# Expert lookup of a hybrid encoder block: one gather of a U row and a V row together instead of two gathers of single rows

## What is computed

```python
        ue = jnp.take(u, it, axis=0)
        act = jax.nn.gelu(jnp.einsum("td,tkd->tk", xt, ue), approximate=False) * gt
        ve = jnp.take(v, it, axis=0)
        return jnp.einsum("tk,tkd->td", act, ve)
```

## Time and profile before

| | before |
|---|---|
| median of 3 runs | 1613.03 us (1610.24 to 1615.33) |
| the profiled execution, its own time | 1609.72 us |
| its span, first to last instruction | 1607.5 us |
| TensorE busy | 1523.1 us (95%) |
| DVE busy | 1426.0 us (89%) |
| ACT busy | 633.5 us (39%) |
| POOL busy | 705.5 us (44%) |
| moved by DMA | 448.19 MB |
| POOL's queue q0 (the gathers) | 57344 packets, 201.42 MB |

### The profile page before, as it was taken

How to read it: one execution, slowest core, us unless ns; L and a number is a source line. 1 busy time by engine, 2 the same in 40 slices (tenths; PEclk the granted TensorE clock), 3 DMA queues, 4 the chain that set the end, 5 groups by cost and what they waited for, 6 DMA issues and landing times.

```text
span 1607.5 us, 22474 instructions
## 1 busy us (share of the span) xinstructions
PE 1523.1 (95%) x7627; PEld 1243.6 (77%) x7627; DVE 1426.0 (89%) x2813; ACT 633.5 (39%) x950; POOL 705.5 (44%) x535
## 2 busy tenths in 40 slices
PE   5999999999999999989999999899899999999997
PEld 3787774675557799978888888788788888888885
DVE  6888876773999899968999999999999999999995
ACT  4235554232113566653333333333233333333333
POOL 0000000001555620006777677677666677778740
PEclk8999999989999999999999999999999999999998
DMA  8432214642221166679999999999999999999991
GB/s 349 166 157 79 79 53 173 221 172 89 89 75 53 61 211 210 216 273 386 411 412 387 410 405 412 410 404 411 359 380 404 392 381 412 404 410 410 408 366 53
DMA packets 127309, 448.19 MB, mean 279 GB/s; under 512 B 13825, under 2 KB 34561, under 8 KB 114561
## 3 DMA queue, kind: packets, MB, share of 16 engines
q1 hardware_dynamic: 68448, 243.21, 40.1%
q0 software_dynamic: 57344, 201.42, 31.9%
q10 hardware_dynamic: 1440, 2.62, 0.4%
HBM read 421.44 MB, written 25.69 MB: 278 GB/s over the span
## 4 chain that ended last, share of the span: by engine, by line
PE 49%; DVE 34%; DMA 6%; issue 6%; ACT 3%; POOL 1%; DVEq 0%; SPq 0%; ACTq 0%
PE ps L911 17%; PE ps L682 10%; PE ps L980 9%; PE ps L673 6%; DVE Us L1881 4%; DVE low L1946 3%; DVE low L1869 3%; PE ps L838 3%; DVE Vs L1898 3%; DMA low<-pu,eidx 3%; DVE low L1911 2%; DVE big L1911 2%; DVE low L1862 2%; DVE As L1902 1%; ACT Vs L1367 1%
## 5 line engine op out<-in xcount | busy, mean ns | idle before, releaser
L911 PE MATMUL ps<-xs,Us 128*128 128x320 f32 x2832 | 452.3, 317 | 42.6 <-DVE Us L1881 40.7
L980 PE MATMUL ps<-Vs,As 128*128 128x512 f32 x2032 | 491.9, 396 | 0.8 <-DVE As L1902 0.8
L911 PEld LDWEIGHTS ps<-xs,Us 128*128 128x128 f32 x2832 | 431.6, 193 | 68.0 <-issue 42.8
L980 PEld LDWEIGHTS ps<-Vs,As 128*128 128x128 f32 x2032 | 388.8, 193 | 75.7 <-issue 1.7
L609 POOL DMA_INDIRECT big<-pv,eidx x192 | 306.9, 1598 | 119.3 <-issue 43.3
L609 POOL DMA_INDIRECT big<-pu,eidx x96 | 141.1, 1469 | 206.0 <-DMA gmat<-big 146.8
L609 POOL DMA_INDIRECT low<-pu,eidx x96 | 147.9, 1540 | 56.8 <-DVE colv L1911 35.5
L1898 DVE TENSOR_TENSOR Vs<-big,Vs 128x1024 fp32r<-128x1024 f32 x127 | 154.9, 1220 | 14.1 <-ACT Vs L1367 14.0
L563 POOL TENSOR_TENSOR xs<-big,xs 128x320 fp32r<-128x320 f32 x8 | 6.6, 858 | 360.0 <-ACT xs L1215 360.0
L1361 ACT ACTIVATE big<-ps 128x320 f32<-128x320 f32 x96 | 42.1, 439 | 296.1 <-PE ps L911 296.1
L673 PE MATMUL ps<-big 128*128 128x512 f32 (+1 forms) x416 | 158.7, 540 | 0.0
(11 more groups left out here) (256 smaller groups left out, 2011.0 us busy)
## 6 DMA issues: line engine op xcount, KB each, us to landing
big<-puT SPq DMA_DIRECT2D x128, 512.0 KB, 6.7
big<-pvP SPq DMA_DIRECT2D x64, 1024.0 KB, 9.9
big<-stream SPq DMA_DIRECT2D x31, 1024.0 KB, 5.0
gmat<-big SPq DMA_DIRECT2D x10, 2048.0 KB, 8.6
graw<-gmat SPq DMA_DIRECT2D x30, 512.0 KB, 11.8
low<-wada SPq DMA_DIRECT2D x28, 512.0 KB, 4.7
work<-wada SPq DMA_DIRECT2D x14, 512.0 KB, 5.3
graw<-gmat SPq DMA_DIRECT2D x15, 256.0 KB, 11.7
```

The source lines that it names most:

```text
L911: mm = nc.tensor.matmul(ps[:, 6 + e, 0:ET], a, xs[:, b, k, :], start=(k == 0 and a is hi and b == 0), stop=(k == KT - 1 and a is lo))
L980: mm = nc.tensor.matmul(ps[:, 2 * b + half, :], a, v_parts[:, w, half * T:(half + 1) * T], start=(opens and i == 0), stop=(last and i == l ...
```

## The change

The host puts U and V side by side (`puv`, 8 KB per expert), and one gather fetches both rows of an expert, 128 partitions x 8 KB, into 4 buffers of 8 KB. There are 192 gathers instead of 384, with the same bytes. The rows are spread over blocks 2 to 126 by `rows_by`, one or two in a block (192 in 125 blocks). In its block a row gets its dot first, ahead of `rest_u`; ACT then applies GELU to the block's one or two columns and multiplies each with its gate (`weigh_rows`, between rounding V and rounding the activations); DVE adds the weighted V rows at the end of the block, behind `weigh`. A buffer is free when its V row has been added.

The 64 head rows are now in one group: 64 tokens x 2 halves of their slots on 128 partitions, one copy of the activations, one sum, one fold. Two DMAs instead of 32 rearrange the gates, and two instead of 32 the indices. POOL issues the first two gathers before `all_stored`. `row_weights` goes; a shorter `folds` comes in block 126, behind that block's additions, and TensorE's fold now waits for it. ACT's turns are written out instead of looped.

```diff
-ROWBUF = 8
+ROWBUF = 4
-XTOK = EXT * NEXT
+XTOK = P // 2
+ROW0, ROW1 = 1, 126
...
+        row = [low[:, 0:2 * D], low[:, 2 * D:4 * D], big[:, 6 * D:8 * D], big[:, 8 * D:10 * D]]
...
+        def rows_by(o):
+            return NROWS * min(max(o - ROW0, 0), ROW1 - ROW0) // (ROW1 - ROW0)
...
-            all_stored(pool)
             pool.wait_ge(g_last, 2)
-            for r in range(2 * NROWS):
+            for r in range(NROWS):
+                if r == 2:
+                    all_stored(pool)
                 fetch(r)
...
                     if last and d == BODY - 2:
                         pe.wait_ge(gel_ready, XT + 2)
-                        pe.wait_ge(row_used, NROWS + XTOK)
-                        for q in range(NEXT):
-                            fold_halves(acc_ext[q], gath[q], begins=(q == 0))
+                        pe.wait_ge(row_used, XTOK)
+                        pe.wait_ge(fold_ready, 4)
+                        fold_halves(acc_ext, gath, begins=True)
...
+            def weigh_rows(r0, r1):
+                act.wait_ge(row_dotted, r1)
+                f(dots[:, r0:r1], dots[:, r0:r1], ACT.Gelu).then_inc(row_gelu, r1 - r0)
+                if r0 == 0:
+                    act.wait_ge(ext_here, 16 * 4)
+                    act.wait_ge(gate_copied, 2)
+                act.wait_ge(row_gelu, r1)
+                for r in range(r0, r1):
+                    f(act_w[:, r:r + 1], act_w[:, r:r + 1], ACT.Copy, scale=dots[:, r:r + 1]).then_inc(row_weighed, 1)
...
+            def add_row(r):
+                dve.wait_ge(row_weighed, r + 1)
+                src, w = row[r % ROWBUF][:, D:2 * D], act_w[:, r:r + 1]
+                dst = acc_ext if r < XTOK else acc[:, r % 2, :]
+                before = r if r < XTOK else r - 1
+                if r in (0, XTOK, XTOK + 1):
+                    i = v.tensor_scalar(dst, src, w, None, ALU.mult)
+                else:
+                    dve.wait_ge(row_used, before)
+                    i = v.scalar_tensor_tensor(dst, src, w, dst, ALU.mult, ALU.add)
+                i.then_inc(row_used, 1)
+
+            def folds():
+                dve.wait_ge(row_gelu, NROWS)
+                dve.wait_ge(row_weighed, NROWS)
+                v.memset(gath[:, XTOK:P], 0.0).then_inc(fold_ready, 1)
+                v.tensor_tensor(gath[:, 0:XTOK], ident[:, 0:XTOK], ident[:, XTOK:P], ALU.add).then_inc(fold_ready, 1)
...
+                    for r in range(rows_by(o - 1), rows_by(o)):
+                        dot(r)
                     if nxt % EVERY != EVERY - 1 and o + 1 < XT:
                         i = nxt - nxt // EVERY
                         rest_u(g * LATE + (EARLY + i), i % 2)
                     weigh(g, d)
-                    for r in range(dots_by(o - 1), dots_by(o)):
-                        dot(r)
-                    if o == UB:
-                        row_weights()
-                    for r in range(adds_by(o - 1), adds_by(o)):
+                    for r in range(rows_by(o - 1), rows_by(o)):
                         add_row(r)
-                    if o == XT - 3:
-                        dve.wait_ge(row_used, 2 * NROWS)
+                    if o == ROW1:
+                        folds()
+                        dve.wait_ge(row_used, NROWS)
                         step(v.tensor_tensor(acc[:, 0, :], acc[:, 0, :], acc[:, 1, :], ALU.add))
                         dve.wait_ge(h_here, 16 * (TB + 1))
```

More of the change, by code:

```diff
@@ L214, in build @@
         As = sb("As", [P, 2, 2 * ET], f32r)
-        nrep = [low[:, (2 + q) * D:(3 + q) * D].rearrange("p (k c) -> p k c", k=KT) for q in range(2)]
-        spread_at = big[:, 8 * D:10 * D].rearrange("p (q d) -> p q d", q=2)
+        nrep = low[:, 2 * D:3 * D].rearrange("p (k c) -> p k c", k=KT)
         Us = sb("Us", [P, 2, 2, D], f32r)
@@ L1268, in _ @@
                 f(n_tok[:, half * T:(half + 1) * T], ps[:, 6 + half, :], ACT.Copy).then_inc(side_free, 1)
[L1270 to L1276, removed]
+            f(nrep.rearrange("p k (q t) -> p k q t", q=2),
+              nT[:, :, P:P + XTOK].unsqueeze(2).broadcast_to([P, KT, 2, XTOK]), ACT.Copy).then_inc(spread_ready, 1)
             def gelu_early(n):
@@ L1319, in _ @@
                     f(graw[:, 1, FILLED - 2, :, :], piece[:, pslot(PIECES - 2), 0:GRUN, :], ACT.Copy).then_inc(g_last, 1)
-                if j == 3:
-                    act.wait_ge(idx_ready, 2)
-                    act.wait_ge(gate_copied, 2)
-                    for q in range(2):
-                        f(n_exts[q], spread_at[:, q, :], ACT.Copy).then_inc(ext_ready, 1)
                 if j == 2:
@@ L1908, in dot @@
                 if r == 0:
-                    dve.wait_ge(ext_ready, NEXT)
+                    dve.wait_ge(ext_ready, 1)
                 row_wait(r)
-                v.tensor_tensor_reduce(out=u_row[r % ROWBUF], in0=u_row[r % ROWBUF],
-                                       in1=n_exts[r // EXT] if r < XTOK else n_tok, scale=1.0, scalar=0.0,
-                                       op0=ALU.mult, op1=ALU.add, accum_out=dots[:, r:r + 1]).then_inc(row_used, 1)
-            def row_weights():
-                dve.wait_ge(row_used, NROWS)
-                step(v.memset(acc[:, 0, :], 0.0))
-                step(v.memset(acc[:, 1, :], 0.0))
-                for q in range(NEXT):
-                    step(v.memset(gath[q], 0.0))
-                settled()
-                for q in range(NEXT):
-                    step(v.tensor_reduce(gath[q][:, q * EXT:(q + 1) * EXT], ident[:, :].rearrange("p (h t) -> p t h", h=PH),
-                                         axis=AX.X, op=ALU.add))
-                dve.wait_ge(gelu_ready, 1)
-                dve.wait_ge(ext_here, 16 * 2 * PH * NEXT)
-                step(v.tensor_tensor(act_w[:, :], act_w[:, :], dots[:, :], ALU.mult))
-                settled()
-                pairs = ident[:, :].rearrange("p (t w) -> p w t", w=2)
-                step(v.tensor_tensor(fold[:, XB:P], pairs[:, 0, :], pairs[:, 1, :], ALU.add))
-                step(v.memset(fold[:, 0:XB], 0.0))
-                settled()
@@ L1935, in add_row @@
[L1935 to L1947 removed]
+                u = row[r % ROWBUF][:, 0:D]
@@ new lines, in dot @@
+                v.tensor_tensor_reduce(out=u, in0=u, in1=n_ext if r < XTOK else n_tok, scale=1.0, scalar=0.0,
+                                       op0=ALU.mult, op1=ALU.add, accum_out=dots[:, r:r + 1]).then_inc(row_dotted, 1)
+            def add_row(r):
[9 more added lines that the diff above has]
+                i.then_inc(row_used, 1)
```

108 lines of the change are left out of this document (30 added, 78 removed).

## The result

The changed kernel takes 1672.55 us (median of 4 runs, 1669.21 to 1677.51), the kernel before 1612.68 in the same comparison (4 runs, 1610.24 to 1615.33): a ratio of 1.038, interval [1.0351, 1.0408]. It is 60 us slower, and outside the predicted range of 1588 to 1640. The profiled execution has a span of 1670.7 us, 63.2 more than before.

What follows compares the result with a forecast made beforehand. DVE's work was taken to set the pace, with TensorE 0.2 us per block behind and gathers just hidden. Seven steps sum to -8.1 us: 1601.6 for a profiled execution, about 1605 for the median; range 1588 to 1640.

Steps and rivals of the forecast that it cites:

- Step 1: Building the matrix: two ACT copies of the head activations go, and DVE's idle time behind them; -2.0 us.
- Step 2: Start of the dense blocks: the first two gathers, issued earlier, compete with the awaited U slice; +4.5 us.
- Steps 3 and 4: Block 62 to 63 without row_weights -5.0, shorter folds +0.9; fewer waits between additions -5.0, rows spread to block 126 -5.
- steps 4 and 5: Dense blocks: row work gains -5.0 by fewer addition waits and -5 by spreading; ACT's single-column work costs +4.
- Step 5: ACT between rounding V and the activations: GELU and single-column multiplications can delay the low part; +4 us, bounds 0 and 9.
- Step 6: The end: three folds go, -4.9, but TensorE idles about 6 us and then loses 2.4; together -2.5 us.
- Step 7: Second row of a two-row block: gather lands in 7.3 us against 7.8 available; +2 us, bounds 0 and 62.
- Rival B: Dot of a two-row block's second row: the buffer loop decides, DVE waits every pair; 1640 or about 1630 us; chance 0.31.
- C: SP's loads: U slices come late beside rows with larger packets; about 1630 us; chance 0.06.
- D: Dense blocks: DMA was the hidden bound, so fewer row bytes per block save 21 us; about 1589 us; chance 0.13.

Runs made afterwards that it cites:

- e_stored: The changed kernel with all gathers behind the wait for the last stores, as before the change; 1676.32 us, ratio 1.039.
- e_onegroup: The kernel before with only the 64 head rows made one group on 128 partitions; gathers, buffers and row_weights stay; 1608.47 us, ratio 0.997.
- e_freedot: The changed kernel with a buffer free at the row's dot and additions reading a resident tile instead of the V row; 1591.74 us, ratio 0.988.
- e_2211: The changed kernel with rows spread 2, 2, 1, 1 by block modulo four instead of 1 and 2 in turn; 1639.29 us, ratio 1.016.
- e_late: The changed kernel with dots behind `rest_u` and the gate product, and ACT's GELU of a row behind its rounding of A; 1638.66 us, ratio 1.015.
- e_all: The changed kernel with rows 2, 2, 1, 1, six buffers from row 84, and dots behind `rest_u` and the product; 1602.94 us, ratio 0.994.

## Why the prediction was wrong, step by step

*Step 1, building the matrix, -2.0.* The store that ends it came at 706.28 instead of 707.40: -1.1. But without the two copies it also came at 708.67 (e_stored) and 711.62 (e_onegroup), so no gain is shown. The idle time that I took for their price did not go with them: DVE still idled 3.37 us at that place, against 3.18.

```profile
559.36 1.23 DVE L1821 TENSOR_TENSOR Us<-big,Us 128x1024 fp32r<-128x1024 f32 x1 [3.37 <-ACT Us L1212]
```

*Step 2, the start, +4.5.* Right in size: 17.0 us from the store to the U slice instead of 13.1, +3.9, and 4.4 by e_stored. Giving it back gained nothing in the total; why is open (e_stored).

*Steps 3 and 4, row_weights and the rows.* From block 62 to 63 it was -3.8, and in e_freedot, where nothing waits for a row, 1134.13 - 1127.12 = 7.01 us, -4.8 against 11.78: as predicted. In e_freedot the other blocks from 3 to 125 gained 10.6 and 4.2 us, 14.8 together, more than the 10 less 4 of *steps 4 and 5*. How it divides between the head additions, the spreading and ACT was not tried.

*Step 5, ACT, +4.* The single columns took 0.2 us for the GELU and 0.3 or 0.48 for the products, and DVE waited for ACT 13.5 us in 26 places for the high part of V, much as in the traces without them (before: 13.1 in 29, e_onegroup: 12.8 in 25). No cost showed.

*Step 6, the end, -2.5.* One fold instead of four, and from block 125 to the end -3.5, which takes in a part of the slack of block 126. The sum of this step is not sound as written: -4.9 for three folds and 2.4 for slow matmuls make the -2.5, and the pause of 6 us itself is put at nothing. The pause was 2.31 us, and the matmuls behind it ran at their usual pace:

```profile
1647.60 1.96 PE L965 MATMUL ps<-big 128*128 128x512 f32 x4 [2.31 <-DVE colv L1901]
1648.99 1.49 PE L958 MATMUL ps<-Vs,As 128*128 128x512 f32 x4
```

*Step 7, the loop of four buffers, +2: this step failed.* Its place was right (the second row of a two-row block), and so was one side of its comparison: 7.8 us available by my sum, 7.5 to 8.1 at the median in the changed kernel. The other side was wrong: I took a landing of 7.3 us, and the 45 rows that DVE waited for took 7.7 to 12.5, 9.7 at the median and 10.4 at the tightest place. I argued that the queue is short when this row is asked for, because few gathers are in flight, and put the loads of U and V that fall on it at +2. But the queue is not filled by gathers alone. Slices of U and V and the routing matrix are asked for in the same few microseconds, and in the blocks where they are, 29 of 31 second rows came late, with 69.5 of the 79.7 us. The row to take was the other one of the same group, the median of 10.5 us in the loaded queue, which I had in hand and explained away. It gives the direction, a landing 2.7 us above the time available, and with it B. It does not give the size: 2.7 us in each of 62 pairs would be 167.

The bookkeeping of blocks 3 to 125, by DVE's timeline:

| | us | DVE idle for rows | DVE idle for other things | the rest: DVE at work |
|---|---|---|---|---|
| before | 832.7 | 8.7 | 18.8 | 805.2 |
| changed kernel | 896.9 | 79.7 | 25.6 | 791.6 |
| e_freedot | 813.1 | 0 | 26.1 | 787.0 |
| e_2211 | 868.1 | 74.0 | 2.2 | 792.0 |
| e_late | 864.1 | 56.1 | 20.3 | 787.7 |
| e_all | 826.8 | 10.0 | 26.4 | 790.4 |

The changed kernel is 83.8 us longer than e_freedot: 79.7 in waits for rows, -0.5 in other waits, and 4.6 in DVE at work. Of these an estimated 3 us are lost overlap, since an operation of 1.22 us starts 1.15 after the one before it except across a wait, and there are 45 of them. The slow matmuls behind a stall would have to show as more waiting for ACT, and do not. And the change did save DVE work, 13.6 us against before.

*Rival B* had the mechanism. Its price, 0.6 us in every pair, was too low and in the wrong form: the waits are up to 4.7 us long, 1.8 in the mean, and come in about a third of the blocks (43 of 123), those with SP's loads ahead of their row. *C* did not occur (ACT waited 1.1 us for U slices), but it is what comes next: 35.9 us in e_freedot. *D* had the right size for what lies beneath: without the waits for rows the kernel is at 1591.7, near its 1589, with full queues. That may be luck: DVE's own work fell by 18.2 us against before and its idle time by 1.4, so the traces do not show that DMA had been the bound. I named waits of over 10 us as what would make the prediction wrong; they were 79.7.

On the Trainium skill's fit ("DMA: Bandwidth & Descriptors", in the section "Anatomy of one DMA — SWDGE (gpsimd) path"), which makes an estimate of 4.4 us for a 1 MB gather: the fastest of 192 in e_freedot took 5.4 us and the median 10.0, so in these queues no gather came as fast as the fit, and it is no price.

## What to carry to other kernels

Before two short-lived buffers are merged into one that is held longer, compare landing plus hold to the last use with the time in which as many rows as there are buffers go by, and take the landing at the median of the loaded queue. Look at what the other queues are asked for just before: here the rows behind the V and routing loads were the late ones. Where the sum is short, more buffers and a shorter hold each gave part of it back here; another order of the rows gave as much by making other waits go away. To price a wait, compare all idle time of the engine that sets the pace, since one wait can take the place of another.

## What the runs showed that I had not expected

- In a stage with a mean of 351 GB/s the rows waited for took 9.7 us at the median and up to 12.5, hardly less than the 10.5 of single rows before at 411 GB/s. The load came in bunches of some 25 us with gaps of 2.5 to 5.
- Splitting a 1 MB gather into two of 512 KB, with everything else kept, made the first half arrive no earlier in effect: 91.5 us of waits instead of 78.5.
- Another order of the same rows left the waits for rows as they were (74.0 us instead of 78.5) and removed nearly all others (2.2 instead of 25.6); the kernel was 33 us faster.
- Landing times grew with the number of buffers, up to 18.4 us with six, while the kernel got faster. A landing time alone says nothing of a cost.
